# A hybrid attention layer on one core: score and value products in two passes on 128-row operands, and a causal mask added by VectorE

## The reference

```python
proj = h @ w_in                      # q, three k, three v, gates, u, v, merge gates
# 8 heads of 64, in 2 groups g of 4 heads r; every group has its own k and v
s_c = einsum(q, kc);  p_c = masked_softmax(s_c, cmp_end <= t);  o_cmp = p_c @ vc   # 31 compressed blocks
s_s = einsum(q, k_sel); p_s = masked_softmax(s_s, causal);      o_sel = p_s @ v_sel
s_w = einsum(q, k_win); p_w = masked_softmax(s_w, causal);      o_win = p_w @ v_win
out = gate0 * o_cmp + gate1 * o_sel + gate2 * o_win
```

## Time and profile before

| | |
|---|---|
| median of 3 runs | 815.35 us (813.4 to 816.27) |
| span of the profiled execution | 811.7 us, 10090 instructions; the median lies 3.65 us above it |
| PE busy | 790.8 us, 97% |
| DVE / ACT / POOL busy | 380.4 (47%) / 300.6 (37%) / 103.7 us (13%) |
| granted PE clock | 0.996 of full |

### The profile page before, as it was taken

How to read it: one execution, slowest core, us unless ns; L and a number is a source line. 1 busy time by engine, 2 the same in 40 slices (tenths; PEclk the granted TensorE clock), 3 DMA queues, 4 the chain that set the end, 5 groups by cost and what they waited for, 6 DMA issues and landing times.

```text
span 811.7 us, 10090 instructions
## 1 busy us (share of the span) xinstructions
PE 790.8 (97%) x3933; PEld 649.6 (80%) x3933; DVE 380.4 (47%) x591; ACT 300.6 (37%) x461; POOL 103.7 (13%) x139
## 2 busy tenths in 40 slices
PE   7999999999999999999998999999999999999995
PEld 6888778777777777788887988888888888888884
DVE  3422694565656566556568422222222242322565
ACT  3413546244545555473334322333322232222321
POOL 2418330011213132200002000000000000000011
PEclk9999999999999999999999999999999999999998
DMA  9334225301012010243360243223333322222201
GB/s 255 129 98 139 59 73 165 99 23 52 9 45 53 1 53 0 52 156 103 116 222 26 67 141 103 81 78 100 103 103 103 103 103 80 80 100 103 103 27 78
DMA packets 57169, 72.77 MB, mean 90 GB/s; under 512 B 3856, under 2 KB 44336, under 8 KB 57136
## 3 DMA queue, kind: packets, MB, share of 16 engines
q1 hardware_dynamic: 57136, 72.32, 27.9%
HBM read 70.21 MB, written 2.10 MB: 89 GB/s over the span
## 4 chain that ended last, share of the span: by engine, by line
PE 93%; DVE 3%; issue 1%; ACT 1%; DMA 1%; POOL 0%; POOLq 0%; SPq 0%; ACTq 0%; DVEq 0%
PE ps L1130 87%; PE ps L1137 4%; PE ps L1368 2%; DVE wl L790 1%; DMA arena<-in_x 1%; DVE stat L1014 0%; ACT wh L545 0%; POOL y L535 0%; DVE y L1039 0%; DVE ptl L794 0%; ACT pth L548 0%; ACT y L731 0%; DVE pcmp L823 0%; POOLq L105 0%; DVE first_l L794 0%
## 5 line engine op out<-in xcount | busy, mean ns | idle before, releaser
L790 DVE TENSOR_TENSOR wl<-stage,wh 128x2048 fp32r<-128x2048 f32 (+1 forms) x50 | 113.6, 2273 | 212.4 <-ACT wh L545 212.4
L545 ACT CAST wh<-stage 128x2048 fp32r<-128x2048 f32 (+1 forms) x50 | 93.8, 1877 | 201.2 <-PE ps L1130 197.8
L1130 PE MATMUL ps<-wh,xh 128*128 128x512 f32 (+1 forms) x384 | 148.2, 386 | 1.4 <-DVE atl L830 1.3
L1130 PE MATMUL ps<-wh,xl 128*128 128x512 f32 (+1 forms) x384 | 146.9, 383 | 0.0
L1130 PE MATMUL ps<-wl,xh 128*128 128x512 f32 (+1 forms) x384 | 146.9, 382 | 0.0
L1130 PE MATMUL ps<-ath,wh 128*128 128x512 f32 (+1 forms) x384 | 146.1, 380 | 0.0
L1130 PE MATMUL ps<-atl,wh 128*128 128x512 f32 (+1 forms) x384 | 146.0, 380 | 0.0
L1130 PE MATMUL ps<-ath,wl 128*128 128x512 f32 (+1 forms) x384 | 146.0, 380 | 0.0
L1130 PEld LDWEIGHTS ps<-wh,xh 128*128 128x128 f32 x384 | 72.5, 189 | 15.8 <-issue 1.5
L1130 PEld LDWEIGHTS ps<-wh,xl 128*128 128x128 f32 x384 | 72.4, 189 | 13.9
L1130 PEld LDWEIGHTS ps<-wl,xh 128*128 128x128 f32 x384 | 72.6, 189 | 13.6
(11 more groups left out here) (228 smaller groups left out, 1063.8 us busy)
## 6 DMA issues: line engine op xcount, KB each, us to landing
stage<-in_w_in SPq DMA_DIRECT2D x28, 512.0 KB, 4.6
stage<-in_w_ffn_gate SPq DMA_DIRECT2D x22, 512.0 KB, 4.7
stage<-in_w_ffn_up SPq DMA_DIRECT2D x22, 512.0 KB, 4.4
stage<-in_w_ffn_down SPq DMA_DIRECT2D x22, 512.0 KB, 3.9
stage<-in_w_out SPq DMA_DIRECT2D x8, 512.0 KB, 4.3
arena<-in_x SPq DMA_DIRECT2D x8, 256.0 KB, 5.6
stage<-in_w_in SPq DMA_DIRECT2D x8, 256.0 KB, 5.8
stage<-in_w_branch_nsa SPq DMA_DIRECT2D x4, 512.0 KB, 6.1
```

The source lines that it names most:

```text
L545: act.copy(wh[:, slot, 0:n], stage[:, slot, 0:n]).then_inc(w_hi, 1)
L790: dve.tensor_tensor(wl[:, slot, 0:n], stage[:, slot, 0:n], wh[:, slot, 0:n].bitcast(fp32), ALU.subtract).then_inc(w_lo, 1)
L1130: return pe.matmul(out, (sh, sh, sl)[i], (mh, ml, mh)[i], start=start and i == 0, stop=stop and i == 2)
```

## The change

- **q high over low.** Each head's transposed q is now a 128-row operand: high part (negated and scaled) in the 64 rows of one half, low part in the other. `ath` holds the four heads of group 0, `atl` those of group 1.
- **k doubled.** k high stands in both halves of a 128-row operand, k low too. One pass with k high gives (q high + q low) by k high, one pass with k low adds the rest: two passes (`mm2`) in place of three. The product low by low is now included.
- **v high beside low.** The stationary operand is the 64 columns of v high and 64 of v low; two passes (probability high, low) give both sums in the two halves of the output partitions; ACT copies the lower one to `obot`, DVE leaves the low part of the upper one in `otop`, and their sum is made by POOL for three tiles and by DVE for the last.
- **Steps.** A pair now holds two heads of one group. Only the first pair of a group has a compressed transpose, of all four heads at once (128x128); both pairs use it, each through a zero-padded value operand `vz`.
- **Mask.** The causal matmul is gone. The scores are negated; DVE adds a mask from SBUF and takes the row minimum in one instruction (`tensor_tensor_reduce`), which also writes the masked scores into `prob`; ACT's exponential now reads `prob`. The next scores wait for the minimum (`s_max`), no longer for the exponential.
- **Before the loop.** The transposes of k and q stand between the row tiles of the last projection chunk; their ACT and DVE parts are 64-row instructions, twice to four times as many; the norm of the gating branch comes later on DVE; the v operands are made by POOL after the second stage buffer is free.
- **Memory.** The new v operand `vs` lies where the second stage buffer was, so in the loop all merge units and the first branch unit come through one stage buffer: each load waits for the low part of the unit just before. The second branch unit (U_BRANCH+1) is loaded after the last value product.

```diff
-        stage = sb("stage", [P, 2, 2048], fp32)
+        stage0 = sb("stage0", [P, 2048], fp32)
+        stage1 = sb("stage1", [P, 2048], fp32, lent)
+        vs = sb("vs", [P, 2048], f32r)
...
-        STEPS = [(qt, pp, br) for qt in TILE_ORDER for pp in range(PAIRS) for br in range(3)]
+        STEPS = [(qt, g, pr, br) for qt in TILE_ORDER for g in range(G) for pr in range(2) for br in range(3)]
-        PT_BANKS = [1 if br == 2 else (qt + 2) // 2 for qt, pp, br in STEPS]
+        PT_BANKS = [1 - pr if br == 2 else (qt + 2) // 2 for qt, g, pr, br in STEPS]
...
-            with sp.Fori(0, (N_MERGE - 2) // 2) as i:
-                for b in range(2):
-                    load(2 * i + U_FILL0 + b, b, rows8(w_in_d, b, 512 * i + C_MERGE + 256 * (2 + b)))
+            for v in range(N_FILL):
+                u = U_FILL0 + v
+                load(u, 0, rows8(w_in_d, 0, C_MERGE + 256 * (2 + v)), u if v else None)
...
+            load(U_BRANCH, 0, nsa_rows(0), U_BRANCH)
+            sp.wait_ge(pv_done, N_STEPS)
+            load(U_BRANCH + 1, 1, rows4(sgu_d, 1, 0, 0, 512))
... ACT
-                    if a >= 2:
-                        act.wait_ge(pt_done, PT_BEFORE[SOFT_STEPS[a - 2] + 1])
-                        act.activation(prob[:, a % 2, g, 0:n], ps[:, g, 0:n], ACT.Exp, bias=nmax[:, a % 2, g:g + 1],
-                                       accum_out=rsum[:, a % 2, g:g + 1]).then_inc(s_exp, 1)
+                        p = prob[:, a % 2, hh, 0:n]
+                        act.wait_ge(s_max, 2 * a + hh + 1)
+                        act.activation(p, p, ACT.Exp, bias=nmax[:, a % 2, hh:hh + 1], scale=-1.0,
+                                       accum_out=rsum[:, a % 2, hh:hh + 1]).then_inc(s_exp, 1)
... DVE
-                        dve.tensor_reduce(nmax[:, a % 2, g:g + 1], ps[:, g, 0:P * (STEPS[i][0] + 1)], AX.X, ALU.max,
-                                          negate=True).then_inc(s_max, 1)
+                    if a >= 2:
+                        dve.wait_ge(pt_done, PT_BEFORE[SOFT_STEPS[a - 2] + 1])
+                        dve.tensor_tensor_reduce(out=prob[:, a % 2, hh, 0:n], in0=ps[:, hh, 0:n], in1=mask[:, SEQ - n:SEQ],
+                                                 scale=1.0, scalar=-NEG, op0=ALU.add, op1=ALU.min,
+                                                 accum_out=nmax[:, a % 2, hh:hh + 1]).then_inc(s_max, 1)
... PE
+            def mm2(out, stationary, mh, ml, start, stop):
+
+                pe.matmul(out, stationary, mh, start=start, stop=False)
+                return pe.matmul(out, stationary, ml, start=False, stop=stop)
...
+            def operands(kh, m):
+                for t in ((0, 1), (2,), (3,), (4,), (5,), (6,), (7,), ())[MT * kh + m]:
+                    operand(t)
+            tokens(U_U, xh, xl, SG, bank_free(4), operands)
...
-                            last = mm3(out, v_t(ath, br)[:, kt, :], v_t(atl, br)[:, kt, :], pth[:, c], ptl[:, c],
-                                       br == 0 and kt == 0, False)
+                            last = mm2(out, v_t[:, br, kt, g, :, :], pth[:, c], ptl[:, c],
+                                       br == 0 and kt == 0, False)
...
-                        mm3(ps[:, g, 0:n], q_t(ath)[r, pp, tok], q_t(atl)[r, pp, tok], k_t(ath, br)[r, 0:n],
-                            k_t(atl, br)[r, 0:n], True, False)
-                        pe.matmul(ps[:, g, n - P:n], ident_r[:, :], causal[:, :], start=False,
-                                  stop=True).then_inc(s_done, 1)
+                        mm2(ps[:, hh, 0:n], q_t(g)[:, 2 * pr + hh, P * qt:P * qt + P], k_t(ath, br, g)[:, 0:n],
+                            k_t(atl, br, g)[:, 0:n], True, True).then_inc(s_done, 1)
```

More of the change, by code:

```diff
@@ L321, in build_layer @@
         QUARTERS = [[] for _ in range(N_STEPS + 3)]
-        for v in range(N_FILL):
+        for v in range(N_FILL - 1):
             end = next(i for i in range(N_STEPS + 3) if fills_done(i + 1) >= 2 * v + 2)
@@ L341, in _, with load @@
         def _(sp):
-            def load(u, slot, parts):
-                sp.wait_ge(w_lo, u - 1)
+            def load(u, slot, parts, lo=None):
+                sp.wait_ge(w_lo, u - 1 if lo is None else lo)
                 for dst, src in parts:
@@ L462, in _ @@
                                pattern=[[0, 4], [-1, P]], channel_multiplier=1).then_inc(masks_ready, 1)
+            pool.wait_ge(xt_done, KD)
+            step(pool.memset(mask, 0.0))
+            pool.affine_select(out=mask[:, SEQ - P:SEQ], in_=mask[:, SEQ - P:SEQ], compare_op=ALU.is_ge, fill=-NEG,
+                               base=0, pattern=[[-1, P]], channel_multiplier=1).then_inc(masks_ready, 1)
             pool.wait_ge(trig_ready, 1)
@@ L695, in _ @@
                     if quarter == 0:
-                        act.wait_ge(w_arrived[u % 2], 32 * (u // 2))
+                        act.wait_ge(w_arrived[0], arrived(u)[1])
                         act.wait_ge(w_used, u - 1)
                     part = slice(512 * quarter, 512 * quarter + 512)
-                    last = act.copy(wh[:, u % 2, part], stage[:, u % 2, part])
+                    last = act.copy(wh[:, u % 2, part], stage[0][:, part])
                     last.then_inc(quarter_hi if quarter < 3 else w_hi, 1)
@@ L742, in _ @@
             ht_hi_of(1)
[L743 removed]
+            late_split(U_FFN + 1, 1)
             root(3)
@@ L945, in lo_quarter @@
                 part = slice(512 * quarter, 512 * quarter + 512)
-                last = lo(wl[:, u % 2, part], stage[:, u % 2, part], wh[:, u % 2, part])
+                last = lo(wl[:, u % 2, part], stage[0][:, part], wh[:, u % 2, part])
                 if quarter == 3:
@@ L1165, in _, with tokens @@
                     last.then_inc(w_used, 1)
-            def tokens(u, lh, ll, n, before):
+            def tokens(u, lh, ll, n, before, after=None):
                 for kh in range(2):
@@ L1180, in tokens @@
                             last.then_inc(rows_done, 1)
-                    last.then_inc(w_used, 1)
+                        if m == MT - 1:
+                            last.then_inc(w_used, 1)
+                        if after:
+                            after(kh, m)
             def bank_free(c):
```

457 lines of the change are left out of this document (272 added, 185 removed).

## The result

The changed kernel takes 777.16 us (median of 4 runs, 776.19 to 778.27) against 815.59 (813.4 to 816.27) beside it on the same chip: ratio 0.9545, 95% interval 0.9522 to 0.9567. The forecast was 777. The profiled spans went from 811.7 to 775.4 us. Of the 36 executions of the kernel before beside the experiments, 22 took 812.3 to 814.1 us at a mean granted clock of 0.996 or 0.997, and 14 took 815.1 to 816.1 at 0.994; the profiled one, at 0.996, is like the 22.

The account below looks back on a forecast made before the run. PE, busy 97% of the span, was taken as the bound. Loop -38.7, before it +0.5, end +0.5 sum to -37.7: span 811.7 to 774.0, median 3.65 higher, about 777 us; forecast 770 to 785 (48%), range 761 to 794 (about 80%).

Parts of the forecast that it names:

- PE's work, 50.7 less: Attention loop: scores save 35.5, values 9.6, compressed step 5.6 us; without PE waits the loop would take 134.6 us.
- 35.5: Loop's score products: two passes per head take 32 steps from 55.7 to 20.2 us, saving 35.5.
- overhead of 0.84: Score step of two heads: 0.84 us beyond six passes, for two small matmuls and changes between 64-row and 128-row operands.
- Waits in the loop, 12: Loop: PE waits on other engines, 8 us from their chain plus 4 us from uneven alternation, giving 146.6 us.
- The lap that I summed: Loop, tile 3: chain of ACT, DVE and POOL work once per triple, 10.6 us against 9.7 of PE's work.
- half-rate rival: Loop: masked minimum runs at half rate, 0.53 us more each at n = 512, 19 us in all; result 796; 17%.
- Before the loop, +0.5: Stretch before the loop: later compression product, GpSimd delay and cheaper compressed scores sum to +0.5 us (from -1.5 to +4).
- The end, +0.5: Behind the loop: loading U_BRANCH+1 late stays hidden; the longer way of the last output costs 0.5 us.
- PE stays dense: Rival for the loop: buffers absorb the chain of DVE, ACT and POOL, loop 134.6 us, result 765; 25%.
- Weights come late: Rival: fills wait 3 to 5 us for each of six units, result 797 to 807; 6% together with no effect.
- The clock fell: Clock rival: PE's waits in tiles 3 and 2 bring 1.2 instead of 2.4 GHz, 73 us more, 850; 4%.
- The 3.65: Whole kernel: the median lies 3.65 us above the profiled span, taking 774.0 to about 777.

Follow-up runs that it names:

- e4: Kernel before with only the mask change: no causal matmul, VectorE adds the mask and takes the row minimum, scores keep three 64-row passes; 785.54 us against 813.39.
- e1: Changed kernel with k low passed twice in each of the 64 score products, three passes in place of two; 777.20 us.
- e2: Changed kernel without the k low pass in the 64 score products, one pass in place of two; 777.24 us.

## Why the prediction was right, point by point

The forecast of 777 came true, and its main step did too: PE loses about 50 us of work in the loop, and the waits on the other engines give about 12 back. Several terms were off and cancelled, and the agreement within 0.5 us is luck.

- **PE's work, 50.7 less.** PE's busy time fell by 49.5, from 184.2 to 134.65. It agrees with the forecast of 134.6 only because 50.7 was taken off the length of the loop, 185.3, which held 1.1 us of idle. The scores saved 33.1 by the table above, not 35.5: a step costs 0.71 us on average and not 0.63, as the first pass behind other work takes about 0.1 more; at n = 512 it is 1.01 where I had put 0.9. The other products must then have saved 1.2 more than I had priced; that I did not trace. The reason was off too: I had put 35.5 us down to fewer passes and half of the overhead of 0.84 to the causal matmuls and the changes of rows. e4 shows that removing the causal matmul does all of it, by letting the two heads run side by side.
- **Waits in the loop, 12.** They are 12.2 us, and by tile (length less PE's busy time) 4.5, 3.5, 2.8 and 1.3 in the tiles 3, 2, 1 and 0, where the prediction's terms give 4.8, 4.0, 2.8 and 0. But the mechanism was only half right. I had two of the three releasers; the third, DVE's `pcl`, ends 3.9 us of the waits. I set the tiles 3, 2 and 1 at 10.6, 9.3 and 7.8 us per triple; measured are 10.86, 10.91 (with the tail) and 7.99. The lap that I summed ran through both branches' extremes and held 0.44 us of PE's work; the real one runs through one softmax, the third iteration's fills and the values, with 4.4 us of PE's. That the wrong lap came within 0.3 us of the right one in tile 3 is luck. In tile 2 I left out the 1.2 us of weight quarters on DVE. The forecast that PE and chain take turns (the larger of the two) was confirmed by e1 and e2 beyond what I then expected of them.
- **DVE.** The masked minimum at full rate was right and the half-rate rival is out. Its read was mis-sized: I took 0.19 us from ACT's accumulator, it is 0.083 and overlaps the next instruction. So DVE's busy time in the loop, forecast to grow from 108.3 to about 115, fell to 99.5. Its groups of instructions add up to 112.4 us (114.2 before), but they now follow one another more closely: 12.9 us of them overlap, 5.9 before.
- **Before the loop, +0.5.** Eight profiles with this same code ahead of the loop have its start between 161.44 and 163.45, mean 162.7; the two with the kernel before's, 161.34 and 161.61. So about +1.2. The product started near the forecast (119.4; 120.57 in this profile), but PE's wait ahead of it was forecast at 2 to 3 us and is 4.0, and the fall of the clock behind it, 1.5 us, I had looked for only in the loop. The delay by GpSimd that I had counted at 1 us costs PE nothing: it has no other wait there. It is there all the same, and mostly on GpSimd's side. Two of its four casts for the v operands took 2.53 and 2.46 us (the others 0.40), while DVE made low parts from SBUF, one of which took 2.70 us for 2.29; the norm's four-column instructions took 0.16 to 0.17.
- **The end, +0.5.** It is 0.0.
- **Rivals.** "PE stays dense" fails by 12.2 us of idle. "Weights come late" fails: no wait on a DMA in the loop. The clock fell, but before the loop and for 4 us only.
- **The median.** The sum of the prediction gives 774.0 + 3.65 = 777.65, and the profiled span came out at 775.4. The 1.4 us missed are +0.3 in the loop, +1.6 before it and -0.5 at the end. The 3.65 made up for them: every execution listed with both numbers lies 1.66 to 1.79 us above its span. So the kernel before's profile, 811.7, is of an execution of 813.4 us, while its median of three was 815.35; 2 of the 3.65 us are the difference of two executions. The changed kernel's median lies 1.8 above its profiled span. With 1.7 the same sum would have given 775.7, 1.5 us short: luck again.

## What to carry to other kernels

Once PE has lost enough work, look for the closed lap through all engines, its own queue included, and change the order of what is on it. In the tiles that such a lap set, some 8 us of matmuls more or less (48 passes) that were not on it changed the time by 0.2 us at most, but for one fall of the clock. Two laps of nearly equal length can hide each other's gains, so edits of single links should be tried together as well as alone. That such edits add up to more than their parts is likely from the waits that moved, and not shown. Before making 64-row products into 128-row ones, look whether two of them can stand next to each other with nothing of 128 rows between.

## What was not expected of the hardware

- Two 64-row matmuls in different halves of the partitions and in different PSUM banks start together: six passes of n = 512 take 0.90 us, 0.15 each, where a 128-row pass of 512 takes 0.23.
- A 128x128 matmul behind each head's passes cost 0.57 us ((1.86 - 0.72) / 2), not the 0.11 of a pass of 128 columns, since it also keeps the two heads apart.
- VectorE's read of its accumulator takes 83 ns and hides under the next instruction; ACT's takes 186 to 194.
- Waits of PE of 1.67, 2.6, 3.75 and 4.0 us each went with about 3 to 4 us at half clock; one of 1.73 did not, and once the clock fell with no wait ahead.
